# Four layers of two transformer blocks as one straight program: no layer loop, no barrier between layers

## The reference

```python
h = rms_norm(x, attn_norm_g[l])
proj = h @ w_in[l]                                   # 1024 x 4768
c_q, c_kv, k_rope, gq, gk, gv, pool_in, gate_logits = split_columns(proj, IN_SIZES)
merged = gates0*(mla(...) @ w_mla) + gates1*(gqa(...) @ w_gqa) + gates2*(pool(...) @ w_pool)
x = x + merged @ w_out[l]
hf = rms_norm(x, ffn_norm_g[l])
u = depthwise_conv(hf @ ffn_w_up[l], ffn_conv_w[l], ffn_conv_b[l])
x = x + (silu(u_gate) * u_val) @ ffn_w_down[l]       # 2816 wide
```

## Time and profile before

| | |
|---|---|
| median of 3 runs | 1835.01 us (1831.6 to 1836.45) |
| the profiled execution | 1830.64 us, of it span 1828.9 us |
| PE / PEld busy | 1632.7 / 1290.0 us (89% / 71%) |
| DVE / ACT busy | 1094.5 / 746.4 us (60% / 41%) |
| moved by DMA | 422.58 MB, mean 231 GB/s |
| mean granted PE clock | 0.956 of 2.4 GHz |

### The profile page before, as it was taken

The page is one execution under the profiler, slowest core; times in us unless marked ns, Lnnn a source line. Parts: engine busy times, 40 slices in busy tenths (PEclk is TensorE's granted clock), DMA queues, the critical chain, the costliest instruction groups (busy, mean ns, idle before and its releaser), DMA issues.

```text
span 1828.9 us, 26214 instructions
## 1 busy us (share of the span) xinstructions
PE 1632.7 (89%) x10562; PEld 1290.0 (71%) x10562; DVE 1094.5 (60%) x1542; ACT 746.4 (41%) x972; POOL 0.2 (0%) x4
## 2 busy tenths in 40 slices
PE   6999989997999989996999898868779999897775
PEld 6877789996877779995887676434467767654433
DVE  5966767787876768775578573222255975522224
ACT  3556445453556545552445632101034565311111
POOL 0000000000000000000000000000000000000000
PEclk9999999998999999998999999989889999898898
DMA  7543355544552435552644298999956337899996
GB/s 240 179 161 115 127 184 184 197 148 158 190 184 92 173 118 205 183 199 67 219 148 144 88 413 348 414 422 415 413 165 206 127 108 276 314 415 420 415 420 251
DMA packets 174258, 422.58 MB, mean 231 GB/s; under 512 B 15968, under 2 KB 68552, under 8 KB 157512
## 3 DMA queue, kind: packets, MB, share of 16 engines
q1 hardware_dynamic: 174152, 421.07, 62.1%
HBM read 419.99 MB, written 1.05 MB: 230 GB/s over the span
## 4 chain that ended last, share of the span: by engine, by line
PE 27%; DMA 15%; DVE 5%; issue 2%; SPq 2%; ACT 2%; DVEq 0%
PE lot L310 5%; PE lot L311 5%; PE lot L312 5%; PE lot L2202 4%; DMA raw<-w_exp_up 3%; DMA two_e_sqT<-w_exp_up 3%; DMA e_lo<-w_exp_up 3%; DMA e_hi<-w_exp_down 3%; SPq L2099 2%; PE lot L2172 2%; PE lot L2276 1%; DMA raw<-w_out 1%; DMA two_e_gates<-w_exp_up 1%; DMA two_e_pt<-w_exp_gate 1%; PE lot L2229 1%
## 5 line engine op out<-in xcount | busy, mean ns | idle before, releaser
L269 DVE TENSOR_TENSOR w_lo<-raw,w_hi 128x2048 fp32r<-128x2048 f32 (+4 forms) x196 | 436.1, 2230 | 133.5 <-ACT w_hi L264 132.9
L264 ACT ACTIVATE w_hi<-raw 128x2048 fp32r<-128x2048 f32 (+4 forms) x196 | 365.0, 1867 | 141.9 <-PE lot L312 116.4
L310 PE MATMUL lot<-one_hT_hi,w_hi 128*128 128x256 f32 x704 | 201.3, 286 | 5.5 <-DVE one_hT_lo L417 5.5
L311 PE MATMUL lot<-one_hT_lo,w_hi 128*128 128x256 f32 x704 | 201.0, 286 | 0.0
L312 PE MATMUL lot<-one_hT_hi,w_lo 128*128 128x256 f32 x704 | 200.9, 285 | 0.0
L310 PE MATMUL lot<-w_hi,two_hT_hi 128*128 128x512 f32 (+1 forms) x448 | 181.3, 405 | 10.8 <-DVE w_lo L269 6.8
L311 PE MATMUL lot<-w_lo,two_hT_hi 128*128 128x512 f32 (+1 forms) x448 | 176.7, 394 | 0.0
L312 PE MATMUL lot<-w_hi,two_hT_lo 128*128 128x512 f32 (+1 forms) x448 | 176.4, 394 | 0.0
L310 PE MATMUL lot<-w_hi,one_hT_hi 128*128 128x512 f32 (+2 forms) x384 | 148.6, 387 | 5.4 <-DVE w_lo L269 2.9
L312 PE MATMUL lot<-w_hi,one_hT_lo 128*128 128x512 f32 (+2 forms) x384 | 145.2, 378 | 0.0
L311 PE MATMUL lot<-w_lo,one_hT_hi 128*128 128x512 f32 (+2 forms) x384 | 145.0, 378 | 0.0
(11 more groups left out here) (442 smaller groups left out, 3241.0 us busy)
## 6 DMA issues: line engine op xcount, KB each, us to landing
raw<-w_in SPq DMA_DIRECT2D x78, 1024.0 KB, 4.9
raw<-ffn_w_up SPq DMA_DIRECT2D x44, 1024.0 KB, 5.1
raw<-ffn_w_down SPq DMA_DIRECT2D x22, 1024.0 KB, 4.8
raw<-w_out SPq DMA_DIRECT2D x16, 1024.0 KB, 5.8
raw<-w_exp_gate SPq DMA_DIRECT2D x14, 1024.0 KB, 18.0
raw<-w_exp_up SPq DMA_DIRECT2D x14, 1024.0 KB, 20.8
two_e_gates<-w_exp_up SPq DMA_DIRECT2D x12, 1024.0 KB, 19.1
e_lo<-w_exp_up SPq DMA_DIRECT2D x10, 1024.0 KB, 21.9
```

Of the source, the lines that this page charges most:

```text
L264: act.activation(K.hi[:, r, 0:n], self.raw(name)[:, 0:n], ACT.Copy).then_inc(K.sig["hi_ready"], 1)
L269: dve.tensor_tensor(K.lo[:, r, 0:n], self.raw(name)[:, 0:n], K.hi[:, r, 0:n].bitcast(F32), ALU.subtract).then_inc(K.sig["lo_ready"], 1)
L310: pe.matmul(out, a[0], b[0], start=start, stop=False)
L311: pe.matmul(out, a[0], b[1], start=False, stop=False)
```

## The change

1. **No loop, no barrier.** `block_one` is built twice, with the layer as a constant, and yields five parts (`sync`, `tensor`, `scalar`, `vector`, `gpsimd`), like `block_two`. All four layers stand in one `nc.Block`. Semaphores are never cleared: each wait adds what the earlier layers have counted (`sig.at(name, n)`, from the tables `ONE_COUNTS` and `TWO_COUNTS`).
2. **The ring goes on.** `Stream` starts with the slots and last chunks of the layer before, so the first chunks of a layer are loaded, and its first one split, in the last steps of the layer before.
3. **First norm of block one by row tiles.** Each tile has its own statistics, root, scaling and 8 transposes; `lat` is multiplied tile by tile.
4. **Last sums by half tiles.** PE signals (`last_half`) when the first 512 columns of a last addend are done. The next layer's DVE program adds them (`add_last`), in block one each half followed by its statistics.
5. **Rotation tables in layer one.** Their seven loads and that of `rope` stand in SP's queue after chunk `pool1`; the angles stand on DVE before the low part of `pool0`; the sines on ACT before the high part of `g4a`. The tables have memory of their own, above the tiles of both blocks.
6. **The start.** `x` is loaded in two tiles; nothing waits for `rope` at the start.

```diff
+def rms_var(K, dve, link, tag, t):
+    mean, var = moments_of(K, dve, link, t)
+    ...
+def rms_scale(K, dve, link, tag, t, out, gain):
+    dve.wait_ge(K.sig[f"{tag}_root"], K.sig.at(f"{tag}_root", t + 1))
+    link(dve.reciprocal(inv, K.stat[:, 2 + t:3 + t]))
+    ...
 class Stream:
-        last = [None] * RING
+        last = list(before.last) if before and goes_on else [None] * RING
+        self.first = first = before.next if before and goes_on else 0 if before else START_SLOT
 block_one, sync:
+            if tables and name == "pool1":
+                sp.dma_start(K.rope[:, :, :], A["c_rope"]).then_inc(sig["rope_in"], 16)
+                load_tables(nc, A, sig, tables, sp)
 block_one, tensor:
-            transpose_x(K, L, pe, M.tmp, ("xT0", "xT1"), sig["n1_normed"])
-            project(K, L, ST, pe, "lat", ("lat0", "lat1"), LATENT, hT, turned=("xT0", "xT1"))
+        transpose_tile(K, L, pe, M.tmp, "xTt0", 0, sig, "n1_normed")
+        L.wait_drained(pe, "xTt0")
+        first_part(0, 0)
+        transpose_tile(K, L, pe, M.tmp, "xTt1", 1, sig, "n1_normed")
+        first_part(0, 1)
+        L.wait_drained(pe, "xTt1")
+        first_part(1, 0)
+        first_part(1, 1)
 block_one, scalar:
-            root_act(K, act, "n1")
+        act.activation(st[:, 232:233], K.ident[:, 0:1], ACT.Sqrt)
             ST.hi_to(act, "lat0")
-            act_hi(K, L, act, "xT0", flat(M.hT_hi[:, 0:4, :]))
-            act_hi(K, L, act, "xT1", flat(M.hT_hi[:, 4:8, :]))
+        root_act_of(K, act, "n1", 0)
+        ST.hi_to(act, "lat1")
+        root_act_of(K, act, "n1", 1)
+        tile_hi(0)
+        tile_hi(1)
...
+        if tables:                       # after the takes of kv0, kv1
+            rotation_sines(sig, tables, act)
 block_one, vector:
+        if before:
+            ST.lo_to(dve, "lat0")
+        first_stats(0)                   # add_last and stats_of, two halves each
+        rms_var(K, dve, link, "n1", 0)
+        rms_scale(K, dve, link, "n1", 0, M.tmp, M.gain)
+        first_stats(1)
+        rms_var(K, dve, link, "n1", 1)
+        ST.lo_to(dve, "lat0")
+        tile_lo(0)
+        rms_scale(K, dve, link, "n1", 1, M.tmp, M.gain)
+        ST.lo_to(dve, "lat1")
+        tile_lo(1)
...
+        if tables:                       # after the low part of cT
+            ST.lo_to(dve, "ukv")
+            rotation_angles(K, sig, tables, dve, link)
             ST.lo_to(dve, "pool0")
 block_two, sync:
+            if ahead and name == "iq1":
+                ahead.L.wait_drained(sp, f"Y{FF_STEPS - 1}t1")
 block_two, tensor:
+            ahead.L.wait_drained(pe, f"Y{FF_STEPS - 1}t0")
+        transpose_tile(K, L, pe, K.x, "xTt0", 0, x_sig, x_normed)
+        if ahead:
+            ahead.L.wait_drained(pe, f"Y{FF_STEPS - 1}t1")
+            transpose_tile(K, L, pe, K.x, "xTt1", 1)
 block_two, vector:
+        if ahead:
+            ST.lo_to(dve, "ik")
+            for t in range(T):
+                for c in range(2):
+                    ahead.add_last(dve, link, t, c)
             tile_lo(dve, 0)
 build:
-            with nc.Fori(0, DEPTH) as layer:
-                block_one(K, one, layer)
-                nc.all_engine_barrier(sems_to_clear=K.sig.span())
-            rotation_tables(K, two)
-            nc.all_engine_barrier(sems_to_clear=K.sig.span())
+        one0 = block_one(K.layer(), one, 0, tables=two)
+        one1 = block_one(K.layer(ONE_COUNTS), one, 1, one0)
+        two0 = block_two(K.layer(ONE_COUNTS, ONE_COUNTS), two, 0, ahead=one1)
+        two1 = block_two(K.layer(ONE_COUNTS, ONE_COUNTS, TWO_COUNTS), two, 1, before=two0, out=out)
```

More of the change, by code:

```diff
@@ L209, in __init__ @@
                 continue
[L210 to L213, removed]
+            r = (j + first) % RING
+            slot[r] += 16
             ready += 1
-            self.landed[n], self.ready[n], self.before[n] = slot[raw], ready, last[r]
-            self.raw_slot[n] = raw
-            self.raw_free[n] = (self.ready[last[r]] if last[r] else 0) if q < RING else ready - 4
+            self.landed[n], self.ready[n], self.before[n] = slot[r], ready, last[r]
+            self.raw_free[n] = last[r][0].ready[last[r][1]] if last[r] else 0
             if n not in ends:
@@ L342, in signals, with layer @@
         return self
-    def layer(self, n):
+    def layer(self, *stages):
         K = Layer()
@@ L1027, in block_one @@
     order += ffn_lots(FF_STEPS)
-    L = Lots(order, K.filled, K.drained)
-    ST = Stream(K, L, names, ONE_WIDTHS, ONE_ENDS | ffn_ends(FF_STEPS), {}, FFN_TURN, {},
-                by_pool=())
+    L = Lots(order, K.filled, K.drained, before and before.L)
+    ST = Stream(K, L, names, ONE_WIDTHS, ONE_ENDS | ffn_ends(FF_STEPS), FFN_TURN, before and before.ST)
+    stage = Layer()
+    stage.L, stage.ST, stage.sig = L, ST, sig
     K.h = M.conv[:, 1, :, :]
@@ new lines, in rotation_angles @@
+    dve.wait_ge(sig["tables"], 112)
+    dve.tensor_copy(M.tri_r[:, :], M.tri[:, :])
+    link(dve.tensor_copy(st[:, 236:236 + T], M.pos[:, :]))
+    for t in range(T):
+        last = dve.tensor_scalar(M.ang[:, 0, t, :], M.inv[:, :], st[:, 236 + t:237 + t], None, ALU.mult)
+    link(last)
+    a, k, c = (M.ang[:, n, :, :] for n in range(3))
+    link(dve.tensor_scalar(k, a, 1.0 / turn, magic, ALU.mult, ALU.add))
+    link(dve.tensor_scalar(k, k, magic, None, ALU.subtract))
+    for part in (c1, c2, c3):
+        link(dve.scalar_tensor_tensor(a, k, -part, a, ALU.mult, ALU.add))
@@ L2474, in norm_dve_of, with block_two @@
            .then_inc(K.sig[f"{tag}_normed"], 1)
-def block_two(K, M, layer, before=None, out=None):
+def block_two(K, M, layer, ahead=None, before=None, out=None):
     nc, A, sig, st = K.nc, K.A, K.sig, K.stat
@@ L3081, in vector @@
         cos, sin = M.rot[:, :, 0:8], M.rot[:, :, 8:16]
-        if before is None:
+        if ahead:
+            ST.lo_to(dve, "ik")
+            for t in range(T):
+                for c in range(2):
+                    ahead.add_last(dve, link, t, c)
             tile_lo(dve, 0)
@@ L3473, in build @@
         one = OneTiles(K)
[L3474 to L3490 removed]
+        two = TwoTiles(K, K.base)
         K.signals(Signals(nc, ctx))
```

1641 lines of the change are left out of this document (807 added, 834 removed).

## The result

The changed kernel takes **1824.84 us** (median of 9 executions, 1821.4 to 1829.84) against 1835.01 of the kernel before: ratio **0.9948, 95% interval 0.9937 to 0.9958**. That is a gain of 10.2 us where 21.5 were forecast, and 1.8 us above the range of 1804 to 1823. Run and profiled a second time, on another chip, it gave a median of 1824.91 against 1834.82, ratio 0.9956 (0.9942 to 0.9971). One execution of this second job took 4088.38 us and one of experiment 9's took 1919.44; both are left out of the medians given here (with them 1826.26 and 1835.96). The spans of its two profiled executions are 1820.0 and 1815.6 us, against 1828.9 before.

What follows compares the result with a forecast made beforehand. PE bounds block one's layers and DMA block two's expert stages, so gains come only at the seams. 1830.64 - 20.5 - 5 + 2 + 3 = 1810.1, with 4.4 for the median 1814.5; predicted 1813.5 us, range 1804 to 1823.

Steps and rivals of the forecast that it cites:

- Second seam, -20.5: Block one into block two: early chunks and half sums end the products at 868.3 instead of 888.8, 20.5 us less.
- I expect no fall: Second seam: TensorE's new pauses near 0.4 and 1.4 us would not bring its clock down to half.
- rival A: Second seam gives only its earlier start, half clock or a late chunk eating 5.9 us: -14.6, 1819.5 us; chance 0.13.
- Start, +2: Program start: lat0 lands at 9.4 us, lat begins at 17.7 but in quarters with gaps, costing 2 us.
- Tables, +3: Layer one: angles wait for table loads behind pool1 and delay pool0's low part, costing 3 us, worst case +5.
- First seam, -5: Between block one's layers: the norm by tiles lets lat end earlier, a gain of 5 us from -6.1 to -4.4.
- t0 ends at 430, its high part at 431: First seam: tile 0's transposes end at 430 us and its high part is ready at 431.
- The half clock that I counted in: First seam: new pauses of 2.8 and 3.7 us may lower the clock, adding 1.7 us to lat.
- B: Tables late and start costing 3: 1817 us; or both costs near nothing, -6 at first seam: 1808; chance 0.17 together.
- C: Whole program: straight code starves engines of instructions, slower than before, 1860 us at one piece in 40 us; chance 0.03.
- D: Second seam: a slot or count keeps the first chunks until the seam, so no prefetch: 1825 us; chance 0.05.
- 4.4 us: Whole program: the runs' median lies 4.4 us above the profiled execution, turning 1810.1 into 1814.5.

Runs made afterwards that it cites:

- experiment 9: Changed kernel, but SyncE waits for block one's last product before loading block two's first chunks, and VectorE's low part of ik stands behind the sums: 1835.61 us, ratio 1.0006.
- Experiment 6: Changed kernel with block one's first norm whole again in both layers, both tiles' sums, roots, scalings and transposes together: 1829.16 us, ratio 0.9959.
- Experiment 1: Changed kernel with ScalarE reordered: tile 0's root ahead of lat0's high part at the start, tile 0's copy ahead of tile 1's root in both layers: 1820.31 us.
- experiment 2: Changed kernel with table loads kept, but angles moved before the first attention maxima and sines before the second norm's table load: 1816.5 us, ratio 0.9922.

## Why the prediction was wrong

The direction and the place were right; three terms of the sum (start, tables, first seam) were too good by 2.4 to 2.8 us each, and the largest, the second seam, came out in one of the two profiles and fell short by 4.3 us in the other.

- **Second seam, -20.5.** Right in its mechanism: 21.0 in one execution. The half sums stand at 851.84 to 856.00 between the products, the chunks are there, and the pause is 1.51 us where I put 1.4. "I expect no fall" is the step that failed as stated. The clock fell in 4 of 7 profiles, which costs 3.2 to 4.8 us: rival A's mechanism, but as a lottery and not as a rule. That no fall would come was read from two seams of one profile: full clock behind 11.00 us of idle time and 16 transposes, half clock behind 12.82 and 3.13 us. Experiment 6 has nearly the pattern of the first, with the half clock behind it, so one seam could not carry it. The Trainium skill's rule that transposes do not count as PE work (TensorE: Matmul & The Clock Gate, Part 4: PE-mode transpose) is not borne out for the float32 transposes of this kernel: 36 of them around block one's norm were followed by the full clock in three of three profiles (1.00 over 2.6 us), against 0.50 in all nine without them. The 12 in the pause of the second seam were followed by 1.00 over 10.2 us in three of three, and so were 14 matmuls in the one profile with them.
- **Start, +2; measured +4.6.** I had seen that the root stands behind lat0's high part, but put lat0 at 9.4 us; it was split from 11.59, behind `x`, the identity and the gain. That is 2.2 us, and the first product came 2.1 us later than the 17.7 I had. The rest is the first products' pace, which I had put between full and half clock: they come every 0.35 us, as at half clock between the layers, and not every 0.19, though the profile's clock reads 1.00 there. Experiment 1 takes 3.8 back.
- **Tables, +3; measured +5.6 to 5.8.** The mechanism is exactly the one written down (experiment 2); its size was that of the worst case and a little more. The last table landed 7.2 us after its issue, where my sum has 2.6 to 4.1: I carried over the 6.2 us from first issue to last landing on an idle queue, although pool1's megabyte stood in front. And SyncE issued them from 45.55, since pool1's release had moved with the start, where I had 40 to 44.4; the terms were worked out as if each stood alone.
- **First seam, -5; measured -2.6.** The step "t0 ends at 430, its high part at 431" failed. I ran down VectorE's queue and not ScalarE's: the copy waits behind tile 1's root for 2.8 us. That gives 1.8 back when mended (experiment 1); the order by tile itself was worth nothing as it stood (experiment 6). The half clock that I counted in did come (0.50 over 4.5 us).
- **Rivals.** B's first half, tables and start worse (1817), is what came, together with part of A; I had them as alternatives, each with a chance, and not as things that can come together. C is refuted: 76 packets of instructions, and layer two takes 398.0 us where it took 398.4. D is refuted by the seam; experiment 9 shows what late chunks cost there, 7.1 us.
- **The way from profile to median.** -8.9 and -13.3 between profiles, -10.2 and -9.9 between medians. I added 4.4 us, the distance of the kernel before; the changed kernel's medians lie 3.0 and 7.5 above its profiled executions. And 1813.5 stands 1 us under the 1814.5 of its own sum, without a reason. A range of 2.5 us either way for executions was too narrow. The second profile's job has eleven like executions of the changed kernel from 1817 to 1833 us, with mean clocks of 0.960 and 0.950 at the two ends.

With start +4.6, tables +5.8, first seam -2.6 and second -21.0 the sum is -13.2, and the second profile shows -13.3; with -16.2 for the second it is -8.4, and the first shows -8.9. The four terms thus hold the whole change in both profiles, since the stretch behind `iq`'s transposes happened to be as long as before in both (906.4 and 906.0 against 906.2).

## What to carry to other kernels

When work is cut into tiles, write down the order of *each* engine's queue at the seam, and ask of each tiny step (a root, a count) which long wait stands before it, and which ready copy stands behind it. Reckon a wait for loads in an engine's queue from the landing of the last of them, on the moved time line and behind what stands ahead of them in the queue; put such work where the engine idles anyway and long after the load. Where a short pause is followed by the half clock in some executions only, one profile can't tell a cause: profile the unchanged kernel twice before you explain.

## What the runs showed of the hardware

The same 1.5 us pause of TensorE behind 16 transposes was followed by up to 10 us at half clock in four profiles and by none in three. Filled, with matmuls or with transposes of a constant, it was followed by the full clock in four of four, which chance alone would do in 11%. Between block one's layers, where the pauses by tile were 2.7 and 3.8 to 5.1 us, and in experiment 6 with its one pause of 5.73 us, the half clock came in all nine profiles without fillers (about 4.5 us for 12 products) and in none of the three with them (2.5 us).

The same 5499 matmuls from `iq`'s transposes to the end took 906.0 to 919.8 us over 13 profiles, with a mean clock of 0.94 to 0.92; the busy times of VectorE and ScalarE there stayed within 0.6 us.

Seven table loads (0.5 MB in all) behind a chunk of 1 MB in one queue: the last landed 7.2 us after its own issue and 10.2 us after the first one's. On an idle queue before the change these were 3.0 and 6.2 us.
